# mLSTM and attention block pair: ScalarE takes the turned quarters out of PSUM, VectorE adds the skip part in SBUF

## The chip, the cores and the metric

The kernel runs on one core of one Trainium2 chip, in one launch. The metric is the device time in microseconds (us); the median of several runs counts. All arithmetic is fp32, and large products are made of three fp32r products of high and low parts.

## The reference

A first block and a second block work on a sequence of 1024 positions of 1024 features. The first block normalises its rows, projects them (`w_in`) to four parts, mixes two of them by windowed means, and runs two of them through a bidirectional mLSTM. Its sum goes through `w_out`. The second block (spatial gating, a wide convolution, windowed attention) is not touched by the change.

The part that the change touches is the mLSTM, cut to what matters:

```
c = silu(conv5(u));  q, k = headwise(c);  v = headwise(u)       # 4 heads of 256 features
for both directions, for chunks of 128 positions, with carried state (C, n, m):
    s   = (q k^T) * exp(log_D - m_t)                            # inside the chunk
    num = s v + inter_w * (q C);   den = rowsum(s) + inter_w * (q n)
    h   = num / max(|den|, exp(-m_t))
    C   = decay * C + (ws * k)^T v                              # to the next chunk
h = h_fwd + h_bwd
h = (h - mean(h)) * rsqrt(var(h) + EPS)                         # over a head's 256 features
out = (h * mh_norm_w + skip_w * c) * silu(m_z)
```

## The kernel before

The mLSTM stage works head after head (`units(h)` on each engine), and in a head over 16 units: unit m is chunk pair p = m // 2 in direction d = m % 2. An engine's order is the order of the Python code of its block; engines wait for each other by semaphores alone, and no planner is involved.

In each unit TensorE makes the state product (inter, L1016, into bank 0), then one item that prepares the next head, then the product inside the chunk (intra, L1026, into four half banks in turn) and the two products of the state update (L1033, banks 2 and 3). The items for the next head are twelve pieces of q (L964), turned k (L974) and v (L976) in units 0 to 11 (`FILL`), and two pieces of scores (L987) in units 12 and 14. They all go through one PSUM bank, bank 1, the fill bank: `fill` waits until the last content of the bank has been taken out.

At the end of units 7, 9, 11 and 13 (`TURN`) TensorE also turns a quarter (128 features by 512 positions) of the head before into feature order (`turn_h`, L1001), for heads 0 to 2 through the same fill bank. The head's 1024 rows have been normalised by then: VectorE gathers statistics, ScalarE makes the root in unit 3 (`root`, L1849, which needs another activation table than the exponentials of `weight`), VectorE the reciprocal in `roots` at the end of the pair of units 4 and 5, and ScalarE normalises two chunks in each of units 5 to 8 (`norm_h`, L2035).

Before, ScalarE writes the skip part (`skip_w * c`) of a quarter into a tile `yt` one unit early (`skip_part`, L2018). VectorE reads the turned quarter from the fill bank, scales it and adds `yt`, at the end of its pair of units (`mix_y`, L1480), after totals (L1517), denominators, outputs and state updates (L1496), and with that frees the bank. GpSimd (POOL) multiplies with the gate (`gate_mul`, L630), ScalarE takes the high part (`high_y`, L2029), and POOL the low part (`gate_low`, L638). Two tiles `yt` are used in turn; whoever writes one first waits for the low part of the quarter two before.

ScalarE's order in a unit, before: weight of the next unit (L2008), a row load on its own DMA queue in odd units (`spread`, four pairs of units ahead), evacuation of the state product into `tmpi` or `tmpj` (L2052), root, norms, high part, skip part, and last the evacuation of the fill bank (L1976 q, L1979 k, L1981 v, L1987 scores). POOL's order: masked weight product `Pm` (L651), weighted keys (L617), a mask for the loaded rows (L623), gate product, low part. SP reloads the gate's tile after each gate product; nothing else on SP stands in the change.

The last head's own quarters (12 to 15) are turned after the stage through other banks; their code keeps its order.

Of the kernel before, what the change touches and what calls it, by code (L numbers as in the profile page):

```python
# [9 lines left out]
ALU = mybir.AluOpType  # L10
ACT = mybir.ActivationFunctionType
# [7 lines left out]
HALF = 512  # L19
# [9 lines left out]
NH = 4  # L29
# [77 lines left out]
def build(nc, I, out):  # L107
# [48 lines left out]
    with ctx:  # L156
# [91 lines left out]
        yts = (yt0, yt1)  # L248
# [81 lines left out]
        def head_quarter(n):  # L330


            return (2 * (n // 4) + n % 2, n % 4 // 2) if n >= 12 else (n // 2, n % 2)

        def yt_last(i):
            return hc0[:, 2 * i:2 * i + 2, :].rearrange("p a b -> p (a b)")
# [427 lines left out]
        def _(pe):  # L764
# [186 lines left out]
            def fill(name, value):  # L951


                turns[0] += 1
                return take(free[turns[0] % len(free)], name, value)
# [35 lines left out]
            def turn_h(h, i):  # L991

                n = 4 * h + i
                mt, nh = head_quarter(n)[0] % 2, head_quarter(n)[1]
                pe.wait_ge(s["v_hn"], NT * h + 4 * nh + 4)
                if h < NH - 1:
                    ps = fill("v_y1", n + 1)
                else:
                    ps = ring_x("v_y1", 12 + 2 * i + 1)
                for b in range(4):  # L1000
                    mm = pe.transpose(ps[:, b * P:(b + 1) * P], hcs[h % 2][:, 4 * nh + b, mt * P:(mt + 1) * P],  # L1001
                                      idn)
                mm.then_inc(s["t_h"], 1)
# [242 lines left out]
        def filled(eng, t_name, t_value, name, value):  # L1246

            eng.wait_ge(s[t_name], t_value)
            return bank[bank_of[name, value]]
# [3 lines left out]
        def _(ve):  # L1253
# [210 lines left out]
            def mix_y(h, i):  # L1464
                n = 4 * h + i
                j = V_MH + head_quarter(n)[0]
                if h == NH - 1:

                    ps = filled(ve, "t_h", n + 1, "v_y1", 12 + 2 * i + 1)
                    ve.wait_ge(s["a_t1"], n + 1)  # L1470
                    y = yt_last(i)
                    ve.scalar_tensor_tensor(y, ps[:, :], VT[:, j:j + 1], y, ALU.mult, ALU.add).then_inc(s["v_y1"], 1)
                    ve.wait_ge(s["v_y1"], 12 + 2 * i + 1)
                    ve.wait_ge(s["l_smz"], 16 * 16)
                    ve.tensor_tensor(y, y, smz_last(i), ALU.mult).then_inc(s["v_y1"], 1)
                    return
                ps = filled(ve, "t_h", n + 1, "v_y1", n + 1)
                ve.wait_ge(s["a_t1"], n + 1)
                y = yts[n % 2][:, :]
                ve.scalar_tensor_tensor(y, ps[:, :], VT[:, j:j + 1], y, ALU.mult, ALU.add  # L1480
                                        ).then_inc(s["v_y1"], 1)

            def state(h, n):
                _, p, d, ck, r = unit(n)
# [49 lines left out]
            def units(h):  # L1534
                for q in range(8 * h, 8 * h + 8):
                    n = 2 * q
                    _, p, _, _, r0 = unit(n)
                    r1 = unit(n + 1)[4]
                    total(h, n)
                    state(h, n)  # L1540
                    total(h, n + 1)
                    if p:
                        ve.wait_ge(s["v_tot"], upd_of(h, p - 1, 1) + 1)
                    sums = wide[q % 2][:, :].rearrange("p (d c) -> p d c", d=2)[:, :, HD]
                    chain(ve.tensor_tensor(den[:, 0, :], sums, cols[:, 1, r0:r1 + 1:r1 - r0], ALU.max))
                    chain(ve.scalar_tensor_tensor(den[:, 0, :], sums, -1.0, den[:, 0, :], ALU.mult, ALU.max))
                    chain(ve.reciprocal(den[:, 1, :], den[:, 0, :]))
                    output(h, n)
                    state(h, n + 1)
                    output(h, n + 1)  # L1550
                    if p >= 6:
                        chunk_mean(n - 4)
                        chunk_mean(n - 3)
                    if p >= 5:
                        chunk_stats(h, n - 2)
                        chunk_stats(h, n - 1)
                    if h and p == 0:
                        head_stats(h - 1)
                    if h and p == 2:
                        roots(h - 1)  # L1560
                    if h and n % 16 + 1 in TURN:
                        mix_y(h - 1, TURN[n % 16 + 1])
                if h == NH - 1:
                    head_stats(h)
# [281 lines left out]
        def _(ac):  # L1846
# [117 lines left out]
            def evac_features(h, i):  # L1964

                if i == 0 and h >= 2:
                    ac.wait_ge(s["t_inter"], 14 * (h - 1))
                    ac.wait_ge(s["g_kw"], 14 * (h - 1))
                    ac.wait_ge(s["t_upd"], 14 * (h - 1))
                    ac.wait_ge(s["t_intra"], 16 * (h - 1))  # L1970
                ps = filled(ac, "t_hw", 12 * h + i + 1, "a_hq", 12 * h + i + 1)
                pv = ps[:, :].rearrange("p (t c) -> p t c", t=2)
                t = 2 * (i % 4)
                if i < 4:
                    m, nh = i // 2, i % 2
                    ac.activation(qTs[h % 2][:, m, nh * HALF:(nh + 1) * HALF], ps[:, :], ACT.Copy  # L1976
                                  ).then_inc(s["a_hq"], 1)
                elif i < 8:
                    ac.activation(kts[h % 2][:, t:t + 2, :], pv, ACT.Copy).then_inc(s["a_hq"], 1)  # L1979
                else:  # L1980
                    ac.activation(vs[h % 2][:, t:t + 2, 0:HD], pv, ACT.Copy).then_inc(s["a_hq"], 1)  # L1981

            def evac_scores(h, b):
                if h >= 2:
                    ac.wait_ge(s["g_P"], 16 * (h - 1))
                ps = filled(ac, "t_st", 2 * h + b + 1, "a_st", 2 * h + b + 1)
                ac.activation(STs[h % 2][:, 4 * b:4 * b + 4, :], ps[:, :].rearrange("p (c t) -> p c t", c=4), ACT.Copy  # L1987
                              ).then_inc(s["a_st"], 1)
# [12 lines left out]
            def weight(n):  # L2001
# [4 lines left out]
                if n >= 2:  # L2006
                    ac.wait_ge(s["g_P"], n - 1)
                ac.activation(Wb[:, n % 2, :], brd(q)[:, d, :], ACT.Exp, bias=cols[:, 3, r:r + 1]  # L2008
                              ).then_inc(s["a_W"], 1)

            def skip_part(n):
                j, nh = head_quarter(n)
                y = yts[n % 2][:, :] if n < 12 else yt_last(n - 12)
                if 1 < n < 12:
                    ac.wait_ge(s["g_ymlo"], n - 1)
                if n == 12:
                    ac.wait_ge(s["t_h"], 12)
                ac.activation(y, cc[:, j, nh * HALF:(nh + 1) * HALF], ACT.Copy,  # L2018
                              scale=VT[:, V_SK + j:V_SK + j + 1]).then_inc(s["a_t1"], 1)

            def high_y(n):
# [16 lines left out]
            def units(h):  # L2038
                weight(16 * h)
                for n in range(16 * h, 16 * h + 16):  # L2040
                    _, p, d, _, r = unit(n)
                    m = n % 16
                    if m < 15:
                        weight(n + 1)
                    if n % 2 and n // 2 + 4 < NU // 2:
                        spread(n // 2 + 4)
                    if p:
                        i = upd_of(h, p - 1, d)
                        ps = filled(ac, "t_inter", i + 1, "a_tmp", i + 1)
                        if n >= 4:  # L2050
                            ac.wait_ge(s["v_h"], n - 3)
                        ac.activation(tmps[p % 2][:, d, :], ps[:, 0:AUG], ACT.Copy, scale=cols[:, 0, r:r + 1]  # L2052
                                      ).then_inc(s["a_tmp"], 1)
                    if h == NH - 1 and m == 15:
                        for k in range(12, 16):
                            skip_part(k)
                    if h and m == 3:
                        ac.wait_ge(s["v_lnv"], h)
                        root(sd[:, :], v1_[:, :])
                    if h and m in (5, 6, 7, 8):  # L2060
                        norm_h(h - 1, 2 * m - 10)
                        norm_h(h - 1, 2 * m - 9)
                    if n in GATE_MUL:
                        high_y(GATE_MUL[n])
                    if h and m + 1 in TURN:
                        skip_part(4 * (h - 1) + TURN[m + 1])
                    if h + 1 < NH:
                        for i in FILL.get(m, ()):
                            evac_features(h + 1, i)
                        if m in (12, 14):  # L2070
                            evac_scores(h + 1, (m - 12) // 2)

            for i in range(12):
                evac_features(0, i)
# [213 lines left out]
```

## Time and profile before

| | us |
|---|---|
| median of 3 runs (1312.31 to 1315.47) | 1312.75 |
| the profiled execution | 1309.26 |
| its span, first to last instruction | 1307.5 |
| TensorE busy in the span | 1228.7 (94%) |
| VectorE busy | 651.2 (50%) |
| ScalarE busy | 349.7 (27%) |
| GpSimd busy | 470.7 (36%) |

Shares over the span mix stages with different limits. The mLSTM units run from about 537 to 745 us of the span; what the change touches is read there. PE is TensorE, PEld its weight load, DVE VectorE, ACT ScalarE, POOL GpSimd.

### The profile page before, as it was taken

The page shows a single profiled execution, that of the slowest core. Times are in us where ns is not written, and L with a number is a line of the kernel's source. Part 1 is how long each engine was busy: PE and PEld are TensorE (multiplying, and loading weights), DVE is VectorE, ACT ScalarE, POOL GpSimd, SP SyncE. Part 2 cuts the span into 40 slices and gives each one's busy share as a digit, 9 for nine tenths or more (in the row PEclk, how much of TensorE's full clock was granted, in tenths as well). Part 3 has the DMA queues.
Part 4 walks back from the last instruction along what each step waited for, and adds up shares of the span by engine and source line. Part 5 has one row for each costly group of instructions (what it writes and reads, how often), then busy time and mean ns, then how long its engine had stood idle before and what let it go on. Part 6 is the DMA issues. An engine that isn't in the chain of part 4 may idle for free.

```text
span 1307.5 us, 17484 instructions
## 1 busy us (share of the span) xinstructions
PE 1228.7 (94%) x6744; PEld 1014.2 (78%) x6744; DVE 651.2 (50%) x1234; ACT 349.7 (27%) x710; POOL 470.7 (36%) x449
## 2 busy tenths in 40 slices
PE   4999999999999999998887999879999999999995
PEld 3777878999888788786666799858988886667784
DVE  5324445311556003375556832871798425445568
ACT  6211111000122112546353611131111134443311
POOL 1123212222446111644444554442313225343433
PEclk9999999999999999999899999889999999999998
DMA  6131121343411132101111262051121210050012
GB/s 207 42 137 41 33 73 33 97 155 104 102 34 47 50 109 83 44 24 34 34 33 37 64 207 65 1 205 33 33 81 48 74 33 33 1 185 33 21 61 113
DMA packets 84484, 92.94 MB, mean 71 GB/s; under 512 B 12721, under 2 KB 72329, under 8 KB 84402
## 3 DMA queue, kind: packets, MB, share of 16 engines
q1 hardware_dynamic: 75698, 87.62, 20.6%
q10 hardware_dynamic: 8704, 4.20, 1.1%
q8 instruction: 55, 0.90, 0.3%
q14 instruction: 27, 0.22, 0.1%
HBM read 74.45 MB, written 18.92 MB: 71 GB/s over the span
## 4 chain that ended last, share of the span: by engine, by line
PE 85%; DVE 9%; issue 2%; ACT 1%; POOL 1%; DMA 1%; SPq 1%; DVEq 0%; POOLq 0%; ACTq 0%
PE bank L790 21%; PE bank L791 20%; PE bank L792 20%; PE bank L1016 3%; PE bank L1033 3%; PE wide L1182 2%; PE wide L869 2%; PE bank L1163 2%; PE wide L1172 2%; PE wide L1026 2%; DVE res L1820 1%; PE bank L987 1%; PE bank L976 1%; DVE Cst L1496 1%; PE bank L964 1%
## 5 line engine op out<-in xcount | busy, mean ns | idle before, releaser
L571 POOL CAST whi<-wraw 128x2048 fp32r<-128x2048 f32 x32 | 61.6, 1925 | 476.6 <-PE bank L792 417.6
L790 PE MATMUL bank<-u_hi,wlo 128*128 128x512 f32 x512 | 201.9, 394 | 3.8 <-DVE u_lo L1285 3.8
L792 PE MATMUL bank<-u_hi,whi 128*128 128x512 f32 x512 | 199.4, 389 | 0.0
L791 PE MATMUL bank<-u_lo,whi 128*128 128x512 f32 x512 | 199.3, 389 | 0.0
L573 POOL TENSOR_TENSOR wlo<-wraw,whi 128x2048 fp32r<-128x2048 f32 x33 | 156.7, 4748 | 2.6
L790 PE MATMUL bank<-x_hi,wlo 128*128 128x512 f32 x320 | 128.8, 403 | 6.2 <-issue 4.5
L791 PE MATMUL bank<-x_lo,whi 128*128 128x512 f32 x320 | 125.8, 393 | 0.0
L792 PE MATMUL bank<-x_hi,whi 128*128 128x512 f32 x320 | 125.7, 393 | 0.0
L790 PEld LDWEIGHTS bank<-u_hi,wlo 128*128 128x128 f32 x512 | 96.3, 188 | 26.3 <-DVE u_lo L1285 4.3
L791 PEld LDWEIGHTS bank<-u_lo,whi 128*128 128x128 f32 x512 | 96.3, 188 | 20.3 <-issue 0.7
L792 PEld LDWEIGHTS bank<-u_hi,whi 128*128 128x128 f32 x512 | 96.2, 188 | 20.3
L790 PEld LDWEIGHTS bank<-x_hi,wlo 128*128 128x128 f32 x320 | 60.7, 190 | 27.4 <-issue 13.6
L736 POOL TENSOR_SCALAR sp<-sp,rcx 128x384 f32<-128x384 f32 (+1 forms) x64 | 35.9, 574 | 112.3 <-DVE rcx L1752 112.3
L790 PE MATMUL bank<-whi,yp_lo 128*128 128x256 f32 x256 | 72.8, 285 | 0.0
L791 PE MATMUL bank<-wlo,yp_hi 128*128 128x256 f32 x256 | 72.4, 283 | 0.0
L792 PE MATMUL bank<-whi,yp_hi 128*128 128x256 f32 x256 | 72.4, 283 | 0.0
L792 PEld LDWEIGHTS bank<-x_hi,whi 128*128 128x128 f32 x320 | 60.8, 190 | 13.2
L791 PEld LDWEIGHTS bank<-x_lo,whi 128*128 128x128 f32 x320 | 60.8, 190 | 11.9
L1665 DVE SCALAR_TENSOR_TENSOR wide<-glu,VT,wide 128x1024 f32<-128x1024 f32 x58 | 69.3, 1282 | 0.0
L790 PE MATMUL bank<-whi,ym_lo 128*128 128x256 f32 x240 | 68.6, 286 | 0.2 <-ACT tmpj L2052 0.2
L791 PE MATMUL bank<-wlo,ym_hi 128*128 128x256 f32 x240 | 68.1, 284 | 0.0
L792 PE MATMUL bank<-whi,ym_hi 128*128 128x256 f32 x240 | 68.0, 283 | 0.0
(321 smaller groups left out, 2541.3 us busy)
## 6 DMA issues: line engine op xcount, KB each, us to landing
wraw<-in_w_in SPq DMA_DIRECT2D x27, 1024.0 KB, 5.4
wraw<-in_w_out SPq DMA_DIRECT2D x12, 1024.0 KB, 5.3
xr<-in_x SPq DMA_DIRECT2D x8, 512.0 KB, 6.8
hst<-in_x SPq DMA_DIRECT2D x4, 1024.0 KB, 5.7
hpool<-hst SPq DMA_DIRECT2D x4, 1024.0 KB, 8.3
smz<-mzs SPq DMA_DIRECT2D x16, 256.0 KB, 2.0
wraw<-nmax ACTq DMA_DIRECT2D x32, 128.0 KB, 3.0
resid<-h SPq DMA_DIRECT2D x8, 512.0 KB, 8.6
```

What stands on the lines that cost most here:

```text
L571: g_.tensor_copy(whi[w % 2][:, :, :], wraw[:, :, :]).then_inc(s["w_hi"], 1)
L573: g_.tensor_tensor(wlo[w % 2][:, :, :], wraw[:, :, :], whi[w % 2][:, :, :].bitcast(F32), ALU.subtract).then_inc(s["w_lo"], 1)
L736: g_.tensor_scalar(row, row, rcx[:, x % 2, i:i + 1], 0.5 if g else 1.0, ALU.mult, ALU.mult).then_inc(s["g_nm"], 1)
L790: pe.matmul(ps, al, bh, start=(k == 0), stop=False)
L791: pe.matmul(ps, ah, bl, start=False, stop=False)
L792: return pe.matmul(ps, ah, bh, start=False, stop=(k == nk - 1))
L869: mm = pe.matmul(ps[:, :], pw[:, g % 2, k, dt * P:(dt + 1) * P], px[:, k, PAD + nh * HALF:PAD + (nh + 1) * HALF], start=(k == 0), stop=(k ...
L1016: mm = pe.matmul(ps[:, 0:AUG], q[:, k, ck * P:(ck + 1) * P], Cst[:, d, k, :], start=(k == 0), stop=(k == 1))
L1026: pe.matmul(ps[:, 0:AUG], Pm[:, n % 2, :], v[:, ck, :], start=True, stop=True).then_inc(s["t_intra"], 1)
L1033: mm = pe.matmul(ps[:, 0:AUG], kwb[:, m % 2, k * P:(k + 1) * P], v[:, ck, :], start=True, stop=True)
L1163: pe.matmul(ps[:, 0:nb * P], qT2[ko:ko + 64, p, n * P:(n + 1) * P], keys[ko:ko + 64, lo * P:(lo + nb) * P], start=True, stop=True).then_in ...
L1665: ins = ve.scalar_tensor_tensor(dst, src, w, acc, ALU.mult, ALU.add)
```

## The change

ScalarE now takes the turned quarters 0 to 11 out of the fill bank with the scale `mh_norm_w` and writes `yt` (`turned_h`), at the end of the unit that turned the quarter. VectorE adds the skip part to `yt`, from `cc` in SBUF, at its old place. ScalarE evacuates the fill bank right behind the state product, ahead of root, norms and high part. The root moves from unit 3 to unit 2, and VectorE's `roots` from the third pair of units to the second. Quarters 12 to 15 keep the old way.

```diff
@@ TensorE, turn_h
-                    ps = fill("v_y1", n + 1)
+                    ps = fill("a_t1", n + 1)
@@ VectorE, mix_y
-                ps = filled(ve, "t_h", n + 1, "v_y1", n + 1)
+                jt, nh = head_quarter(n)
                 ve.wait_ge(s["a_t1"], n + 1)
                 y = yts[n % 2][:, :]
-                ve.scalar_tensor_tensor(y, ps[:, :], VT[:, j:j + 1], y, ALU.mult, ALU.add
-                                        ).then_inc(s["v_y1"], 1)
+                ve.scalar_tensor_tensor(y, cc[:, jt, nh * HALF:(nh + 1) * HALF], VT[:, V_SK + jt:V_SK + jt + 1], y,
+                                        ALU.mult, ALU.add).then_inc(s["v_y1"], 1)
@@ VectorE, units
-                    if h and p == 2:
+                    if h and p == 1:
                         roots(h - 1)
@@ ScalarE
+            def turned_h(n):
+                j = V_MH + head_quarter(n)[0]
+                if n > 1:
+                    ac.wait_ge(s["g_ymlo"], n - 1)
+                ps = filled(ac, "t_h", n + 1, "a_t1", n + 1)
+                ac.activation(yts[n % 2][:, :], ps[:, :], ACT.Copy, scale=VT[:, j:j + 1]).then_inc(s["a_t1"], 1)
+
             def skip_part(n):
                 j, nh = head_quarter(n)
-                y = yts[n % 2][:, :] if n < 12 else yt_last(n - 12)
-                if 1 < n < 12:
-                    ac.wait_ge(s["g_ymlo"], n - 1)
                 if n == 12:
                     ac.wait_ge(s["t_h"], 12)
-                ac.activation(y, cc[:, j, nh * HALF:(nh + 1) * HALF], ACT.Copy,
+                ac.activation(yt_last(n - 12), cc[:, j, nh * HALF:(nh + 1) * HALF], ACT.Copy,
                               scale=VT[:, V_SK + j:V_SK + j + 1]).then_inc(s["a_t1"], 1)
@@ ScalarE, units
+                    if h + 1 < NH:
+                        for i in FILL.get(m, ()):
+                            evac_features(h + 1, i)
+                        if m in (12, 14):
+                            evac_scores(h + 1, (m - 12) // 2)
                     if h == NH - 1 and m == 15:
                         for k in range(12, 16):
                             skip_part(k)
-                    if h and m == 3:
+                    if h and m == 2:
                         ac.wait_ge(s["v_lnv"], h)
                         root(sd[:, :], v1_[:, :])
...
-                    if h and m + 1 in TURN:
-                        skip_part(4 * (h - 1) + TURN[m + 1])
-                    if h + 1 < NH:
-                        for i in FILL.get(m, ()):
-                            evac_features(h + 1, i)
-                        if m in (12, 14):
-                            evac_scores(h + 1, (m - 12) // 2)
+                    if h and m in TURN:
+                        turned_h(4 * (h - 1) + TURN[m])
```

## Rows read from the trace of the kernel before

**Rows 1.** The page's chain that ended last: share of the span by engine.

```profile
PE 85%; DVE 9%; issue 2%; ACT 1%; POOL 1%; DMA 1%; SPq 1%; DVEq 0%; POOLq 0%; ACTq 0%
```

**Rows 2.** Windows, heads 0 to 3: stretch, length, busy by engine, granted clock, DMA.

```profile
536.90:581.00 44.10, 43.85 (x232) 37.38 (x232) 28.80 (x86) 19.21 (x45) 19.79 (x41) 1.00 0.09 25
581.00:643.60 62.60, 51.95 (x248) 42.38 (x248) 35.58 (x107) 30.36 (x64) 28.64 (x48) 0.92 0.12 34
643.60:705.70 62.10, 49.99 (x246) 40.59 (x246) 35.38 (x107) 29.55 (x63) 29.40 (x47) 0.95 0.12 35
705.70:745.40 39.70, 35.01 (x160) 27.98 (x161) 33.13 (x101) 22.23 (x47) 26.62 (x44) 1.00 0.12 34
```

**Rows 3.** Waits in the stage: who for whom, us in total, times, longest.

```profile
PE bank L987 <- DVE yt L1480: 9.0, 4, 2.5
...
PE bank L974 <- ACT kt L1979: 6.0, 2, 3.0
...
PE bank L976 <- DVE yt L1480: 4.1, 4, 1.3
```

**Rows 4.** Timeline of TensorE in head 1, unit 9: start, length, what.

```profile
610.98 1.03 PE L1016 MATMUL bank<-Cst,qT 128*128 128x257 f32 x4
611.85 1.05 PE L976 MATMUL bank<-bdh,um 128*128 128x128 f32 x8
612.74 0.60 PE L1026 MATMUL wide<-v,Pm 128*128 128x257 f32 x2
...
614.04 0.60 PE L1001 MATMUL bank<-cst,hc 128*128 128x128 f32 x4
614.48 1.03 PE L1016 MATMUL bank<-Cst,qT 128*128 128x257 f32 x4
```

**Rows 5.** Timeline of head 1, ScalarE's first norms and VectorE's second add.

```profile
598.49 1.09 ACT L2035 ACTIVATE hc<-hc,nmr,rs 128x256 f32<-128x256 f32 x2 [3.46 <-DVE nmr L1455]
...
616.00 0.74 DVE L1480 SCALAR_TENSOR_TENSOR yt<-bank,VT,yt 128x512 f32<-128x512 f32 x1
```

**Rows 6.** Lines by shape, ScalarE: count, busy us, mean ns, idle before.

```profile
L1864 ACT ACTIVATE u_hi<-wide,VT 128x512 fp32r<-128x512 f32 x16 | 10.4, 689 | 1.9 <-PE wide L843 1.7
...
L1979 ACT ACTIVATE kt<-bank 128x512 f32<-128x512 f32 x14 | 8.3, 590 | 0.0
```

**Rows 7.** Timeline around the root, heads 1 and 3.

```profile
586.54 0.60 ACT L1976 ACTIVATE qT<-bank 128x512 f32<-128x512 f32 x1 [0.38 <-PE bank L964]
...
587.63 0.36 DVE L1509 TENSOR_SCALAR v_<-mv 128x8 f32<-128x8 f32 x1
...
589.20 1.28 ACT L1849 ACT_TABLE_LOAD   x1
...
590.67 1.03 PE L1016 MATMUL bank<-Cst,qT 128*128 128x257 f32 x4
...
712.75 0.63 DVE L1509 TENSOR_SCALAR v_<-mv 128x8 f32<-128x8 f32 x1
...
714.42 0.42 DVE L1517 TENSOR_TENSOR wide<-wide,tmpj 128x257 f32<-128x257 f32 x1
```

**Rows 8.** VectorE at 128x512 (ns min/median/max), POOL's wait and longest operation.

```profile
L1347 DVE TENSOR_TENSOR yp_lo<-yr,yp_hi x16: 679/688/3042, 79.9 to 237.2; 128x512 fp32r<-128x512 f32 x16
...
L1480 DVE SCALAR_TENSOR_TENSOR yt<-bank,VT,yt x12: 730/740/743, 607.9 to 744.3; 128x512 f32<-128x512 f32 x12
...
POOL yt L630 <- DVE yt L1480: 17.1, 10, 2.2
...
L638 POOL TENSOR_TENSOR ym_lo<-yt,ym_hi 128x512 fp32r<-128x512 f32 x11 | 14.2, 1291 | 6.1 <-ACT ym_hi L2029 6.1
```

**Rows 9.** Timeline of head 3: ScalarE's first norms, VectorE's total behind them.

```profile
722.13 1.09 ACT L2035 ACTIVATE hc<-hc,nmr,rs 128x256 f32<-128x256 f32 x2 [3.16 <-DVE nmr L1455]
...
723.98 0.43 DVE L1517 TENSOR_TENSOR wide<-wide,tmpj 128x257 f32<-128x257 f32 x1 [1.88 <-ACT tmpj L2052]
...
726.22 0.43 DVE L1517 TENSOR_TENSOR wide<-wide,tmpj 128x257 f32<-128x257 f32 x1 [1.04 <-ACT tmpj L2052]
```

## The prediction, written before the result was known

> **What bounds the kernel now.** The page comes first: TensorE makes 85% of the chain that ended last [rows 1]. An average over the span says little here, because the change touches one stage only, so the stage is cut by heads, each from its first intra product to the next head's [rows 2]. The reader is to compare the four windows. Head 0, which has neither turned quarters nor row norms, takes 44.1 us, and TensorE is busy in 43.85 of them at full granted clock (1.00): TensorE is its pace. Heads 1 and 2 do the same work plus four turned quarters of the head before and take 62.6 and 62.1 us; TensorE is idle for 10.65 and 12.1 us of them, and its clock is granted at 0.92 and 0.95. Head 3 has no next head to fill and takes 39.7 us.
>
> The list of waits names the idle time [rows 3]: scores (L987) and values (L976) wait for VectorE's L1480, which empties the one fill bank of the turned quarter, 13.1 us in eight waits, and the turned keys (L974) wait 6.0 us in two for a ScalarE evacuation (L1979).
>
> The order of time shows why. TensorE's turn starts at 614.04 [rows 4], VectorE reaches the bank at 616.00 and frees it at 616.74 [rows 5]: 2.70 us, since the add stands at the end of a pair's chain (totals, denominators, states, outputs). And at 598.49 ScalarE has idled 3.46 us in front of two norms, which stand ahead of the key evacuation, so TensorE stands about 3 us (half of the 6.0).
>
> **The change part by part.**
>
> *The bank goes to ScalarE.* Twelve adds of 0.74 us that read PSUM on VectorE become twelve scaled copies that read PSUM on ScalarE, and twelve scaled copies from SBUF (L2018) go there. A scaled PSUM copy of 128x512 is in the trace at 0.69 (L1864), an unscaled one at 0.59 (L1979) [rows 6]. I take 0.69; ScalarE's work in count stays what it is. What counts is when the bank comes free. A unit without a gap gives the pieces [rows 4]: state product (inter) 0.87, fill 0.89, intra and update 1.30, turn 0.44. After the first turned unit's fill ends, TensorE has 1.30 + 0.44 = 1.74 us to the end of the turn, then the next state product of 0.87 in another bank, so the bank is wanted at 2.61. ScalarE evacuates the fill (0.59) and does two norms (1.09 [rows 5]), 1.68, waits for the turn and copies to 1.74 + 0.69 = 2.43. That is 0.18 early, so this edit's wait goes to nothing; the later turns have no norms and more room. Behind the waiting copy stand the next unit's weight, state evacuation and fill evacuation. The weight has a unit's lead (intra needs it about 2 us later), and the other two need TensorE work that also comes after the turn: nothing more waits.
>
> *The fill evacuation moves ahead of root, norms and high parts.* No instruction is added and none issues a DMA. It makes TensorE's release independent of the norms; the norms and the high parts come at most one evacuation (0.59) later, and the consumer of the high part, a POOL subtraction, has a unit of room.
>
> *Root and reciprocal earlier.* VectorE's two small instructions move by a pair of units, so the norms at unit 5 find their factor ready; some 3.3 us of ScalarE idling goes in each head. The root itself moves past one weight, one row load and one state evacuation on ScalarE. The row load is for four pairs on, so no one waits for it. The state evacuation holds the next state product and VectorE's total. In head 1 the root's table load stands at 589.20 now; the evacuation that it will follow ends at 587.14 [rows 7], and VectorE's variance (587.63 + 0.36) is ready before the load ends. So load, root and the load back (2 x 1.28 and about 0.2) end at 589.9, the weight (0.4) follows, and the state evacuation (0.47) ends near 590.7, where the next state product starts now, 590.67 [rows 7]. That leaves nothing, or 1.3 (one table load) if the load only starts once the variance is there; I take 0.3 for each of heads 1 and 2. In head 3 no fill evacuation lies ahead, so the root must wait for the variance at 713.4 (712.75 + 0.63), the load back ends near 714.9, the weight near 715.3, and the state evacuation comes at about 715.2; VectorE's total goes from 714.42 [rows 7] to 715.7. Price 1.3.
>
> *The skip part on VectorE in SBUF.* The operation takes both large operands from SBUF, a form this stage doesn't show at 128x512. The nearest row, L1347, also has two SBUF operands and ranges from 0.68 (median 0.69) to 3.04 [rows 8], so the bounds are 0.06 less than now and, with POOL's longest operation here (1.29, L638 [rows 8]) in the way, 1.3 more. I take the median, 0.69. In heads 1 and 2 it lies beside TensorE's work: a pair with a turn takes TensorE 3.06 + 3.50 = 6.5 us, and VectorE's share of such a head is 35.6 us over eight pairs, 4.4 each [rows 2]. POOL waits for it ten times of twelve, 17.1 us in all [rows 8], so POOL is mostly quiet just then. In head 3 VectorE is the pace (33.1 of 39.7 us busy [rows 2]), so there it is on the path: 4 x (0.69 - 0.74), nothing, up to 4 x 1.3 = 5.2 more if POOL is in the way each time.
>
> The spread of L1347 is a case for a rule. The Trainium skill, "SBUF — State Buffer", section "Who interferes with whom", says that a VectorE instruction with two SBUF inputs contends with a GpSimd instruction that reads SBUF, and that the later one stands until the first is done. The trace agrees in kind (0.68 at best, 3.04 at worst, against adds with one PSUM input, which keep to 0.73 to 0.74 throughout [rows 8]). By row the sum gets nothing for it; by the rule it gets what the third rival below works out.
>
> **The sum.** From first intra product to first intra product head 0 takes 44.1, head 1 62.6, head 2 62.1 [rows 2]. Without the waits heads 1 and 2 are head 0 with four turns: 44.1 + 4 x 0.44 = 45.9, plus 0.3 for the root and 0.2 at the head's end, where the last high part still waits for the last gate product: 46.4. Gains 16.2 and 15.7. These are larger than the named waits because they hold products made at the lower of the clock's two levels after idle stretches (a granted mean of 0.92 in head 1, where TensorE is busy 51.95 us for work worth 43.85 + 1.76 [rows 2]) and the wait at the head's end that follows from a late last add. Head 3: VectorE idles 1.88 us before 723.98 for a state evacuation held by the norms that began at 722.13 [rows 9], and 1.04 before 726.22 [rows 9]; 2.9 goes, 1.3 comes: 1.6. Together 16.2 + 15.7 + 1.6 = 33.5. What follows (the output projection, its loads, POOL's splits) is released by this stage's own semaphores and shifts as a whole. The profiled execution took 1309.26 (span 1307.5): 1275.8. The median of the runs, 1312.75, is 3.5 above it, so I forecast 1279.
>
> **The rivals.**
>
> *Only the named waits go.* The pace in heads 1 and 2 passes to VectorE's chain per pair, which keeps the clock low and the wait at the head's end. For it: 35.6 us of VectorE's work in a head of 46.4 would be 77%, and its steps in a pair depend on one another. Against it: head 0 runs at TensorE's pace with the same chain. Then 9.0 + 4.1 + 6.0 = 19 us [rows 3]: 1294.
>
> *The norms still wait.* The root's own wait and two table loads eat what the earlier place gives; the stalls of L974 and the idling in head 3 stay, 6.0 + 2 of clock and 2: about 10 less, 1289. Against it: the variance is ready more than 10 us before the norms (587.99 [rows 7] against 598.49 [rows 5]).
>
> *Two SBUF inputs meet POOL.* In head 3 POOL is busy 26.6 of 39.7 us, 67% [rows 2]. An add that meets its longest operation of 1.3 waits half of it on average, 0.65; 4 x 0.67 x 0.65 = 1.7: 1281.
>
> *Slower.* ScalarE's queue is in order, and the copy stands behind norms, high parts and their waits. Place: the fill bank after each turn. VectorE frees it now 2.70 us after the turn's start [rows 4, 5]; the copy does so at 0.44 + 0.69 = 1.13 if ScalarE is free. If ScalarE ran 1.6 us late, the bank would gain nothing, and from there each us late costs 8 us over the eight turns of heads 1 and 2. With 3.5 late: 8 x 1.9 = 15 lost against 8 won by the norms, so 1320. Against it: ScalarE is busy 30.4 of 62.6 us [rows 2], and 30.4 of 46.4 is still 65%.
>
> **How the numbers follow.** Forecast 0.70 (its own range 1274 to 1285: 37 us when every TensorE gap goes, 28 with the upper bounds of root and add). Named waits only 0.14, norms still wait 0.02, POOL in the way 0.08, slower 0.06, of which 0.02 near its point of balance with today's time. A measurement of this kernel can tell about 0.3% (4 us) from no change. Faster 0.70 + 0.14 + 0.02 + 0.08 = 0.94, same 0.02, slower 0.04. The range reaches from 1273 to the first rival, 1294.
>
> **What would show it.** Right: no TensorE wait on VectorE's `yt`, none of L974 on L1979; the granted clock of heads 1 and 2 at 0.99 or more; firsts of intra 46 to 47 us apart; ScalarE's copy of the turned quarter at 0.69 and within 1.3 us of the turn's start; no ScalarE wait for `nmr`. Wrong: TensorE waiting at L976 or L987 for ScalarE's `yt` or for VectorE's states; adds far over 0.7 beside POOL; a ScalarE stretch of 2 us or more before the root in heads 1 and 2.

## The result, and the profile after

The changed kernel takes 1283.4 us (median of 4 runs, 1282.51 to 1284.05); the kernel before, run beside it, takes 1312.53 (4 runs, 1311.08 to 1315.47). The ratio is 0.9775, with a 95% interval of 0.9756 to 0.9793: 29.1 us less. The forecast was 1279, with a range of 1273 to 1294.

The profiled execution took 1283.93 us, its span 1282.1. The profile page's chain of waits by engine answers to [rows 1]: VectorE's share falls from 9% to 7%.

```profile
PE 86%; DVE 7%; POOL 3%; issue 2%; ACT 1%; SPq 1%; DMA 1%; ACTq 0%; POOLq 0%; DVEq 0%
```

The windows of heads 0 to 3, with the columns of [rows 2] (stretch, length, busy time and count of PE, PEld, DVE, ACT and POOL, granted clock, DMA share, GB/s):

```profile
540.65:584.78 44.13, 43.86 (x232) 37.39 (x233) 28.82 (x86) 19.23 (x45) 19.81 (x41) 1.00 0.09 25
584.78:632.71 47.93, 46.92 (x248) 38.47 (x249) 35.22 (x108) 30.89 (x64) 29.54 (x48) 1.00 0.15 42
632.71:681.60 48.89, 46.46 (x247) 37.95 (x247) 35.22 (x107) 29.96 (x63) 30.25 (x47) 1.00 0.16 46
681.60:720.09 38.49, 35.09 (x161) 27.88 (x161) 33.00 (x101) 21.74 (x47) 27.93 (x44) 1.00 0.12 36
```

Head 0, which the change doesn't touch, is what it was. Heads 1 and 2 get 14.7 and 13.2 us shorter, head 3 1.2. The stage falls from 208.5 to 179.4 us, and these 29.1 are the whole gain: after the stage both profiles take 562 us (562.1 and 562.0). The two spans differ by 25.4 only because what comes ahead of the stage took 540.65 us in this execution and 536.9 in that of before, in code that is the same.

TensorE's idle time in heads 1 and 2 fell from 10.65 and 12.1 us to 1.0 and 2.4, and the granted clock is 1.00 in both. The waits of the stage (who for whom, us in total, times, longest) that answer to [rows 3] and to POOL's in [rows 8]:

```profile
POOL yt L630 <- DVE yt L1480: 5.9, 5, 1.7
...
ACT yt L2016 <- PE bank L1001: 5.4, 10, 0.8
...
PE wide L1026 <- POOL Pm L651: 4.7, 6, 1.9
...
PEld bank L987 <- issue: 1.7, 4, 0.4
...
PEld bank L976 <- ACT yt L2016: 1.4, 4, 0.4
...
PE bank L1016 <- ACT tmpj L2056: 0.8, 2, 0.5
```

No wait of scores or values for VectorE is left and none of the turned keys. What is left of the fill bank is 1.4 us of weight loads for the values that wait for ScalarE's copy, and 1.7 us in front of the scores' weight loads, for which the profile names no releaser ("issue"). These four loads stand behind the turns of units 11 and 13; in head 1 the first begins at 620.41, 0.11 after the copy's end (619.61 + 0.69), so they are the bank's too. The largest TensorE wait is now that for `Pm`.

The bank's release in the first turned unit of head 1, in order of time (start, length, engine, line), answers to [rows 4, 5]:

```profile
604.82 1.08 ACT L2039 ACTIVATE hc<-hc,nmr,rs 128x256 f32<-128x256 f32 x2
...
605.43 0.60 PE L1001 MATMUL bank<-cst,hc 128*128 128x128 f32 x4
...
605.87 1.03 PE L1016 MATMUL bank<-Cst,qT 128*128 128x257 f32 x4
606.07 0.69 ACT L2016 ACTIVATE yt<-bank,VT 128x512 f32<-128x512 f32 x1 [0.17 <-PE bank L1001]
...
606.81 0.97 PEld L976 LDWEIGHTS bank<-bdh,um 128*128 128x128 f32 x8 [0.31 <-ACT yt L2016]
606.81 1.16 PE L976 MATMUL bank<-bdh,um 128*128 128x128 f32 x8
```

The copy ends at 606.76, 1.33 us after the turn began; VectorE's add ended 2.70 after it. In this unit TensorE gets the bank within a tenth of a microsecond of wanting it (606.81 against 606.74, the state product's start plus 0.87).

### The profile page after: what moved, and what is told of

Its sections match the earlier page's. It is cut to its first block, busy times and chain, and to the rows that moved or that the text cites. A ratio compares the mean times of both kernels' runs of the same rounds, so it can differ in the third digit from the quotient of the medians.

```text
span 1282.1 us, 17482 instructions
## 1 busy us (share of the span) xinstructions
PE 1224.2 (95%) x6744; PEld 1012.1 (79%) x6744; DVE 651.2 (51%) x1234; ACT 350.0 (27%) x710; POOL 473.5 (37%) x449
## 4 chain that ended last, share of the span: by engine, by line
PE 86%; DVE 7%; POOL 3%; issue 2%; ACT 1%; SPq 1%; DMA 1%; ACTq 0%; POOLq 0%; DVEq 0%
PE bank L790 22%; PE bank L791 21%; PE bank L792 21%; PE bank L1016 3%; PE bank L1033 3%; PE wide L1182 2%; PE wide L869 2%; PE bank L1163 2%; PE wide L1172 2%; PE wide L1026 2%; DVE res L1820 1%; PE bank L987 1%; PE bank L976 1%; POOL ym_lo L638 1%; DVE res L1836 1%
```

## The experiments

The theory: TensorE was held in two ways, by the time at which the turned quarter left the fill bank and by norms that stood in ScalarE's queue waiting for a root. The clock's lower level followed from both. Rivals: the order of ScalarE's evacuations is what pays; VectorE's load is what pays (the engine counts, not the time of release); one wait only hid another. Times are medians beside runs of the kernel before on the same chip. A time can tell about 4 us, so smaller effects are read from the heads' lengths in the traces, one trace per run; the heads 1 to 3 together took 164.4 us before and 135.3 after.

**Parts alone, on the kernel before.**

*e1_evac_first: only the evacuation's place.*

```diff
                         ac.activation(tmps[p % 2][:, d, :], ...).then_inc(s["a_tmp"], 1)
+                    if h + 1 < NH:
+                        for i in FILL.get(m, ()):
+                            evac_features(h + 1, i)
+                        if m in (12, 14):
+                            evac_scores(h + 1, (m - 12) // 2)
...
                         skip_part(4 * (h - 1) + TURN[m + 1])
-                    if h + 1 < NH:
-                        (the same block)
```

> The kernel before with one part of the change: ScalarE evacuates the fill bank right behind the state product. VectorE still empties the turned quarter, the root stays in unit 3. My theory: the turned keys of unit 6 no longer wait for the norms, but the next state product does (its evacuation stands behind them), so some 2.5 us in each of heads 1 and 2 and nothing in head 3: 1307.5, with TensorE's 13 us of waits for VectorE's yt unchanged. Rival (the order of the evacuations is what pays): 1290 or less, and the waits for yt shrink.

Measured: 1309.98 beside 1309.55, ratio 0.9996 (0.9977 to 1.0014). Heads 1 to 3 get 2.0 us shorter in all. The waits of its stage show why:

```profile
PE bank L987 <- DVE yt L1480: 9.0, 4, 2.5
...
PE bank L976 <- DVE yt L1480: 5.4, 4, 1.4
PE bank L1016 <- ACT tmpj L2052: 5.0, 4, 1.8
```

The 6.0 us of the turned keys [rows 3] are gone. In their place the state product (L1016) of heads 1 and 2 stands 3.0 us (the other 2.0 of its 5.0 are in head 3 and were there before), and the values wait 1.3 us more for `yt`: the waiting norms now hold the next state evacuation instead of the key evacuation. A wait behind which another engine stands is not cured by changing what stands behind it.

*e2_root_early: only the root and the reciprocal.*

```diff
-                    if h and p == 2:
+                    if h and p == 1:
                         roots(h - 1)
...
-                    if h and m == 3:
+                    if h and m == 2:
                         ac.wait_ge(s["v_lnv"], h)
```

> The kernel before with the root in unit 2 and the reciprocal at the end of the second pair, nothing else. My theory: ScalarE's 10 us of waiting for nmr go, TensorE's 6.0 us at L974 go, and with the clock after them about 5 us in heads 1 and 2 and 1 in head 3: 1301.5; the waits for yt stay at 13 us. Rival (the norms are hidden behind the waits for yt that follow): within 4 us of the kernel before.

Measured: 1300.77, 0.9932 (0.9914 to 0.9950), 8.8 us less; heads 1 to 3 get 11.6 shorter in its trace. Its head 1:

```profile
585.75:642.58 56.83, 49.08 (x248) 39.88 (x248) 35.21 (x108) 30.28 (x64) 28.66 (x48) 0.97 0.13 38
```

The wait of the turned keys on the matmul side is gone, the eight on L1480 stand as they were (9.0 and 4.3). Against [rows 2], TensorE's idle time in heads 1 and 2 falls by 2.9 us each (the named 6.0), its busy time by 2.9 and 1.5, with the granted clock at 0.97 in both instead of 0.92 and 0.95, and head 3 by 1.45.

*e3_both_orders: e1 and e2 together.*

> Everything of the change but the engine: evacuation first and root early, VectorE still empties the bank at the end of its pair. My theory: the two orders solve the same wait, so together they give no more than the early root alone, 1301; what is left to the changed kernel, some 18 us, is the bank. Rival (the order pays): under 1290.

Measured: 1300.67, 0.9926 (0.9905 to 0.9947): e2's time. The two orders deal with the same wait, and the rival that ScalarE's order pays for itself falls. Its heads 1 and 2:

```profile
584.93:641.65 56.72, 48.73 (x249) 40.04 (x249) 35.21 (x108) 30.71 (x64) 28.65 (x48) 0.97 0.14 38
641.65:699.20 57.55, 48.16 (x247) 39.57 (x247) 35.02 (x107) 29.80 (x63) 29.37 (x47) 0.97 0.13 38
```

TensorE still idles 8.0 and 9.4 us, at a granted clock of 0.97: what is left to the changed kernel, 17.2 us in heads 1 to 3, is the bank.

*e4_add_sooner: e3, and VectorE keeps the bank but adds sooner.* The mix stands ahead of the pair's second state update, its second output and the statistics instead of behind them.

```diff
+                    if h and n % 16 + 1 in TURN:
+                        mix_y(h - 1, TURN[n % 16 + 1])
                     state(h, n + 1)
...
-                    if h and n % 16 + 1 in TURN:
-                        mix_y(h - 1, TURN[n % 16 + 1])
```

> As the run with both orders, and VectorE's scaled add from PSUM stands ahead of its second state update instead of at the pair's end, some 1.2 us sooner and ahead of the statistics; the engine and the operation stay. My theory: what counts is when the bank comes free, not which engine does it; the add would end some 1.5 us after the turn's start against 2.7 to 3.8 now, and most of the 18 us come: 1287, waits for yt under 3 us in total. Rival (ScalarE's hand matters, because VectorE's chain is the pace): 1297 or more, with new TensorE waits for VectorE's states (L1496).

Measured: 1288.97, 0.9838 (0.9821 to 0.9856), 20.6 us less. Head 1 and head 3, and head 1's second turn:

```profile
587.42:636.20 48.78, 47.09 (x248) 38.46 (x248) 35.20 (x108) 30.69 (x64) 28.56 (x48) 1.00 0.15 44
...
685.84:725.59 39.75, 35.45 (x161) 27.88 (x161) 32.89 (x101) 21.77 (x47) 27.56 (x44) 1.00 0.12 35
```

```profile
615.02 0.60 PE L1001 MATMUL bank<-cst,hc 128*128 128x128 f32 x4
...
615.81 0.74 DVE L1480 SCALAR_TENSOR_TENSOR yt<-bank,VT,yt 128x512 f32<-128x512 f32 x1
```

The add ends 1.53 us after the turn's start (2.70 before, 1.33 with ScalarE's copy), and heads 1 to 3 take 138.2. So, by the heads' lengths, the two orders (in the main the early root) make 11.9 of the 29.1 us (164.4 to 152.5), the time of release 14.3 (152.5 to 138.2) and the step to ScalarE 2.9 (138.2 to 135.3): turned units of 3.68 to 4.69 instead of 3.89 to 4.98 us, and 1.26 in head 3, where e4's add stands ahead of a state update. This last step also frees the bank 0.20 sooner, so what the engine alone is worth isn't separated. The rival that VectorE's load pays falls for heads 1 and 2: most of the gain comes with the add still on VectorE.

The times split less clearly. They give 8.9 us to e3 and 11.7 more to e4; from e4 to the changed kernel the ratios, taken on two chips (0.9838, and 0.9782 for after_again), leave about 7, good to some 4. Up to 1.7 of that can be head 0 (the last section). So 2.9 may be too low for the last step.

**Parts undone or moved, on the changed kernel.**

*e5_old_root: root and reciprocal at their old place* (the two lines of e2 turned round).

> The changed kernel with the root back in unit 3 and the reciprocal at the end of the third pair. My theory: the norms wait for nmr again, but behind the evacuation of the fill bank, so only the next state product is held: from the unit lengths of the run with the evacuation first alone, 1.9 us more in each of heads 1 and 2 and 1.1 in head 3, so 5 us slower than the changed kernel. Rival (with the bank on ScalarE a late norm also delays the copy of the first turned quarter and the clock falls): 10 us or more slower.

Measured: 1290.73, 0.984 (0.9811 to 0.9870); heads 1 to 3 take 140.1, 4.8 more. Units 3 to 6 of head 1 take 2.60, 3.32, 2.61 and 4.36 us instead of 2.89, 2.90, 2.61 and 2.61. So the early root is worth 4.8 us here, and 9.9 where VectorE empties the bank (e1 against e3, 162.4 and 152.5): in e5 the granted clock of heads 1 and 2 is 1.00, in e1 it is 0.94. What a part is worth depends on the parts that are already there.

*e6_root_unit3: the reciprocal early, the root back in unit 3* (only the line with `m == 2`).

> The changed kernel with the root back in unit 3, but VectorE's reciprocal stays at the end of the second pair. My theory: the early reciprocal is what frees the norms; the root in unit 2 holds the third state evacuation by two table loads and costs 0.6 us in heads 1 and 2 and about 1 in head 3. Back in unit 3 it costs 0.2 per head: 1.5 us faster than the changed kernel, seen in units 3 and 4 of the trace (2.6 and 2.8 us in place of 2.9 and 2.9). Rival: VectorE waits for the later root in its second pair and the units 4 and 5 grow: slower by 1 to 3.

Measured: 1284.31, 0.9794 (0.9775 to 0.9812), not to be told from the changed kernel. Head 3 gains 0.97; its root had waited 0.36 for the variance and no longer does, and the rest of the gain isn't explained. Heads 1 and 2 take 0.13 longer each, with 2.60 and 3.31 in units 3 and 4 instead of 2.89 and 2.90. The gain is half of what I expected: in heads 1 and 2 the two table loads cost the same wherever they stand.

*e10_evac_last: the fill evacuation back behind the high part.* The block of e1, put just ahead of `turned_h`.

> The changed kernel with ScalarE's evacuation of the fill bank back behind root, norms and high part (but ahead of the turned copy, which needs it). My theory: with the early root nothing in front of it waits long; only in unit 7 do the norms make the turn wait 0.45 us, so about 1 us slower than the changed kernel in heads 1 and 2 together. Rival (evacuation first is what lets ScalarE hold the pace): each of the units 5 to 13 grows by the 1.08 of norms or 0.6 of the high part, 10 us or more slower.

Measured: 1285.3, 0.9791 (0.977 to 0.9812); heads 1 and 2 take 0.9 us more together, unit 7 alone 0.57 each. This part of the change is worth 1 us.

*e11_more_vector: one more VectorE operation ahead of each add* (row statistics of the same `cc` quarter, whose result is not used).

```diff
+                q = cc[:, jt, nh * HALF:(nh + 1) * HALF]
+                mark(ve.bn_stats(scr[:, :], q))
                 ve.scalar_tensor_tensor(y, cc[...], ...)
```

> The changed kernel with one statistics operation of 0.7 us more on VectorE ahead of each of the twelve adds; its result is not used. My theory: VectorE's add lies beside TensorE in heads 1 and 2, apart from about 0.6 us at each head's end, and on the path in head 3 (4 x 0.7): 4 us slower in all. Rival (VectorE is near the pace in heads 1 and 2 as well): 0.7 us for each of eight units more, 8 us or more. Second rival (hidden everywhere): no change in any head.

Measured: 1288.89, 0.9811 (0.979 to 0.9831). Heads 1 and 2 take 0.5 us more each, all of it at the head's end; head 3 takes 1.73 more. The start of its head 3 (one line further down in this kernel, L1027 and L1034):

```profile
685.48 0.72 PE L1027 MATMUL wide<-v,Pm 128*128 128x257 f32 x2 [2.36 <-DVE hc L1534]
686.00 1.92 PE L1034 MATMUL bank<-v,kwb 128*128 128x257 f32 x4
```

The state update's products take 1.92 us there and 1.03 in the changed kernel: TensorE is at the lower level of its clock (granted 0.69 from 685.48 to 690.98), and unit 1 takes 0.61 more. So only 1.1 of the 1.73 stand in the units of the adds, where four operations of 0.68 put in 2.7. In heads 1 and 2 VectorE's work lies beside TensorE's but for the last quarter, as forecast; in head 3 it is on the path, but for less than half of its length.

*after_again: the changed kernel once more, for the comparison on this chip.*

> The changed kernel once more, on the same chip as the three others, so that they are compared with it directly. All theories: 29 us faster than the kernel before, with the unit lengths of the first trace (turned units 3.68 to 3.74 and 4.69 us).

Measured: 1284.58, 0.9782 (0.9759 to 0.9806); heads 1 to 3 take 135.3 again.

**Towards a better version.**

*e7_turn_inside: the turn between the two products of the state update* (behind the first, instead of behind the second), so that it ends sooner before the next fill.

```diff
+                            if h and k == 0 and n % 16 in TURN:
+                                turn_h(h - 1, TURN[n % 16])
...
-                    if h and n % 16 in TURN:
-                        turn_h(h - 1, TURN[n % 16])
```

> The changed kernel with TensorE's turn between the two products of the state update. The bank comes free 0.43 us sooner against the next fill. My theory: the turned units of heads 1 and 2 are 0.18 to 0.30 us longer than their products because ScalarE's copy ends just after the fill wants the bank; they go from 3.68 to 3.74 us to 3.50 and from 4.69 to 4.39: 2 us faster in all. Rival (the extra is the matmul's own start after a change of operands, or the state of VectorE): no change in these units.

Measured: 1283.04, 0.9788 (0.9767 to 0.9808). Turned units take 3.60, 3.60, 4.49 and 4.39 us instead of 3.68, 3.68, 4.69 and 4.69, but the head's end takes 0.22 more, since the high part there now waits for the gate product. Head 3 takes 1.7 us longer, at a lower granted clock (the last section).

*e8_weight_first: at a head's end the next weight ahead of the last high part.*

```diff
-                weight(16 * h)
+                if h == 0:
+                    weight(0)
...
+                    if m == 15 and h + 1 < NH:
+                        weight(n + 1)
                     if n in GATE_MUL:
                         high_y(GATE_MUL[n])
```

> The changed kernel with the next head's first weight ahead of the last high part on ScalarE, in unit 15. My theory: the 2.24 and 2.45 us between the last intra product of heads 1 and 2 and the first of the next wait for weight, then POOL's product, and the high part stands ahead with 0.52: these go to about 1.75 and 1.95, 1 us faster in all. Rival (POOL's gate product or low part sets the head's end): no change there, or the second unit of the next head grows by as much.

Measured: 1281.93, 0.9776 (0.9755 to 0.9796); heads 1 and 2 get 0.51 and 0.53 us shorter, which was expected; only the trace can tell it. The order of time at the end of head 1, first the changed kernel, then e8:

```profile
631.04 0.62 ACT L2033 ACTIVATE ym_hi<-yt 128x512 fp32r<-128x512 f32 x1
...
631.56 0.68 ACT L2008 ACTIVATE Wb<-wraw,cols 128x128 f32<-128x128 f32 x2
...
632.20 0.46 POOL L651 TENSOR_TENSOR Pm<-ST,Wb 128x128 f32<-128x128 f32 x1 [0.57 <-ACT Wb L2008]
...
632.71 0.70 PE L1026 MATMUL wide<-v,Pm 128*128 128x257 f32 x2 [0.79 <-POOL Pm L651]
```

```profile
627.71 0.39 ACT L2008 ACTIVATE Wb<-wraw,cols 128x128 f32<-128x128 f32 x1
...
628.00 0.62 ACT L2033 ACTIVATE ym_hi<-yt 128x512 fp32r<-128x512 f32 x1
628.36 0.46 POOL L651 TENSOR_TENSOR Pm<-ST,Wb 128x128 f32<-128x128 f32 x1
...
628.87 0.70 PE L1026 MATMUL wide<-v,Pm 128*128 128x257 f32 x2 [0.27 <-POOL Pm L651]
```

The weight, `Pm` and the first intra product of the next head come half a microsecond sooner once the high part (0.62) no longer stands ahead of the weight.

*e9_all: e7, e8, and the root in unit 3 for the last head alone.*

```diff
-                    if h and m == 2:
+                    if h and m == (3 if h == NH - 1 else 2):
```

> The changed kernel with three edits together: the turn between the two products of the state update, the next head's first weight ahead of the last high part, and the root in unit 3 for the last head only. Where each works on another unit, the savings read from the single runs' units add: 1.4 us in the turned units, 1.0 at the heads' ends (the 0.2 that the turn's place cost there goes too), 1.0 in head 3: 3.4 us faster than the changed kernel on the same chip. Rival (the gaps move to the next wait): within 1.5 us of it.

Measured: 1280.87, 0.9760 (0.9738 to 0.9782). Its heads 1 to 3 take 132.0 us, 3.3 less than in the changed kernel:

```profile
584.30:631.27 46.97, 46.39 (x248) 38.54 (x248) 35.16 (x107) 30.92 (x64) 28.67 (x48) 1.00 0.14 41
631.27:678.89 47.62, 45.83 (x246) 38.02 (x247) 35.26 (x106) 30.67 (x63) 29.47 (x47) 1.00 0.16 46
678.89:716.29 37.40, 34.61 (x160) 28.12 (x161) 33.51 (x102) 21.91 (x47) 27.58 (x44) 1.00 0.14 43
```

Its heads 1 to 3 are the shortest of all traces, and its median is the lowest (e8 has the shorter span, 1278.1 against 1278.9, with head 0 at 44.1 instead of 45.8). Against the changed kernel on the same chip (0.9782, 0.9759 to 0.9806) the intervals overlap, so that it is faster by the time alone isn't shown.

## Why the prediction was right, and where the 4.4 us went

*What bounds the kernel: right.* The two waits named were the two causes: e2 takes the one away, e4 the other, and nothing outside the stage changed.

*Gains larger than the named waits: right.* The first rival (named waits only, 1294) fell with the granted clock: 1.00 in heads 1 and 2 where it was 0.92 and 0.95. Two of the signs named beforehand came out against the forecast, by little: TensorE's loads do wait at L976 for ScalarE's `yt` (1.4 us), and heads 1 and 2 take 47.9 and 48.9 us, not 46 to 47.

*The step that was mis-sized: "That is 0.18 early, so this edit's wait goes to nothing".* The heads 1 to 3 came to 135.3 us where the forecast's own terms make 130.9 (46.4 + 46.4 + 38.1). The difference of 4.4 is that between 1279 and 1283.4, and the units' lengths place it:

| term | forecast | measured | us missed |
|---|---|---|---|
| turned units over 3.50 and 4.39, four each in heads 1 and 2 | 0 | 0.18 to 0.30 each | 2.0 |
| root in units 3 and 4, heads 1 and 2 | 0.3 each | 0.58 each | 0.6 |
| head's end over head 0's 1.73 | 0.2 each | 0.51, 0.72 | 0.8 |
| head 2's first two units over head 0's | 0 | 0.64 | 0.6 |
| head 3 | -1.6 | -1.2 | 0.4 |

The first term: I let the turn end where the next product begins, 0.44 after its start. The row of the turn lasts 0.60 [rows 4], and the copy starts 0.64 after the turn's start (606.07 against 605.43). With that in the working, the copy ends at 1.30 + 0.64 + 0.69 = 2.63, the bank is wanted at 2.61, and the slack of 0.18 was never there. A fill that waits also begins with a weight load that lies beside no earlier product (above, load and product both start at 606.81; in the unit of [rows 4], which has no wait, the load starts at 611.63 and the product 0.22 later). So its eight products take 1.16 instead of 1.05: 0.07 of lateness and 0.11 of that make the 0.18. The four fills of scores begin 1.09 instead of 0.87 after the state product and take 0.08 longer, which makes the 0.30. e7 ends the turn sooner: its scores begin at 0.87 again, and 1.4 of the 2.0 us come back.

The root: the working had the next weight and state evacuation 0.4 and 0.47 behind the second load. In head 1:

```profile
590.91 1.28 ACT L1849 ACT_TABLE_LOAD   x1
...
592.20 0.21 ACT L1849 ACTIVATE sd<-v_ 128x8 f32<-128x8 f32 x1
...
592.43 1.28 ACT L2008 ACT_TABLE_LOAD   x1
...
594.03 0.46 ACT L2056 ACTIVATE tmpj<-bank,cols 128x257 f32<-128x257 f32 x1
594.59 0.43 DVE L1517 TENSOR_TENSOR wide<-wide,tmpj 128x257 f32<-128x257 f32 x1 [1.91 <-ACT tmpj L2056]
```

The load stands ahead of the root's own input, as I worked out (it begins at 590.91, VectorE's variance at 591.39), so the upper end of 1.3 didn't come; but the sequence holds two units by 0.29 each, and VectorE's total by 1.91. The norms (L2039) no longer wait for `nmr` in any head.

The head's end: the last high part stands ahead of the next head's weight, and e8 shows that this is 0.5 of it per head. Head 2's first units wait for `Pm` behind a POOL subtraction; they did so before, and head 0 as the model of a head without waits doesn't have it.

Head 3: 2.9 was to go and 1.3 to come. Unit 6 fell from 4.51 to 2.50, which is 2.0; the early root costs 0.97 (e6). Idle time of VectorE was taken at its full length, where the unit on TensorE got shorter by less.

Two bounds of the forecast's own range don't come out as written, without bearing on the forecast: 37 us less than 1312.75 is 1276, not 1274, and with both upper bounds (2.0 for the root, 5.2 for the adds) 26.3 of the 33.5 are left, not 28.

*The skip part in SBUF: right in kind, 0.05 too low.* The adds take 0.74 in the median, no less than with PSUM (0.69 was taken). The shortest takes 0.732, so the 0.05 is the operation's own length and no meeting with POOL. Such meetings lengthen a few. The lines by form (ns min, median, max) of VectorE's adds and POOL's weighted keys, after:

```profile
L1480 DVE SCALAR_TENSOR_TENSOR yt<-cc,VT,yt x12: 732/741/930, 607.4 to 719.0; 128x512 f32<-128x512 f32 x12
```

```profile
L617 POOL TENSOR_SCALAR kwb<-kt,cols x56: 467/478/1010, 540.6 to 714.6; 128x256 f32<-128x256 f32 x56
```

Before, the adds kept to 730 to 743 [rows 8] and the weighted keys to 498 at most. In order of time, head 3:

```profile
707.05 1.29 POOL L638 TENSOR_TENSOR ym_lo<-yt,ym_hi 128x512 fp32r<-128x512 f32 x1
707.96 0.93 DVE L1480 SCALAR_TENSOR_TENSOR yt<-cc,VT,yt 128x512 f32<-128x512 f32 x1
708.30 0.90 POOL L651 TENSOR_TENSOR Pm<-ST,Wb 128x128 f32<-128x128 f32 x1
```

The add that begins beside POOL's subtraction takes 0.19 longer, and POOL's 0.46 product behind it takes 0.90. A stand to the end of the first one's row would be 0.38 and 0.59; what each takes longer is 0.19 and 0.44. The trace thus agrees in kind with the Trainium skill, "SBUF — State Buffer", section "Who interferes with whom" (VectorE with two SBUF inputs and a GpSimd instruction that reads SBUF hold each other up, the later one standing until the first is done), but the price is small and most of it falls on POOL: five weighted keys of 0.91 to 1.01 and two products of 0.90 and 0.91 make about 3.2 us there. Twelve adds of 774 ns on average instead of 737 make 0.44 us in all. The third rival priced 0.65 per add in head 3; the adds there come to at most 0.93.

*The slower rival fell.* ScalarE's own queue hardly holds the copy: ten of the twelve copies wait for TensorE's turn (5.4 us), among them all eight of heads 1 and 2, and start 0.64 to 0.70 after its start; the other two, in head 3, come straight behind ScalarE's high part, 0.76 after it. In e10 the fill evacuation stands late in its queue again, and that costs 0.9 us over both heads, not the 15 us of this rival.

## What to carry to other kernels

Where one bank passes between engines, write the release as a time after the producer's start, and take the producer's end from its row's length, not from the start of the next one: a slack of 0.18 us on paper was one of -0.02. Look first for what an engine's queue holds while it waits (the norms that waited for a root): making the awaited value earlier paid 8.8 us here (4.8 once the bank came free early), and changing the order behind the wait paid nothing that the time shows. Release time came before the choice of engine: by the heads' lengths 14.3 of the gain, by the times 11.7, could be had by moving one VectorE instruction, on top of the two orders.

## What the runs showed of the hardware that was not expected

*The clock's lower level doesn't follow from the same idle time each time.* Head 0 is the same code in all kernels and took 44.1 us in eight of the fourteen traces and 45.8 in six. TensorE's first products there in the changed kernel, and in its second profile (after_again):

```profile
540.65 0.70 PE L1026 MATMUL wide<-v,Pm 128*128 128x257 f32 x2 [1.93 <-POOL Pm L651]
541.19 1.05 PE L1033 MATMUL bank<-v,kwb 128*128 128x257 f32 x4
542.08 1.02 PE L964 MATMUL bank<-cc,Amat 128*128 128x512 f32 x2
```

```profile
542.54 0.70 PE L1026 MATMUL wide<-v,Pm 128*128 128x257 f32 x2 [1.92 <-POOL Pm L651]
543.08 1.59 PE L1033 MATMUL bank<-v,kwb 128*128 128x257 f32 x4
544.46 1.91 PE L964 MATMUL bank<-cc,Amat 128*128 128x512 f32 x2
```

After the same idle time (1.93 and 1.92 us) the two products of the fill took 1.02 us in one execution and 1.91 in the other, whose granted clock over the head is 0.96 instead of 1.00. That is 1.7 us which belongs to no edit; it is why head 0 is left out of the sums above.

The length of the idle time counts all the same. Taken over the starts of heads 0 and 3 in the fourteen traces, none of the eighteen that follow at most 1.86 us of it is slowed; of the ten that follow 1.90 to 2.36 us eight are (their first two units take 0.6 to 2.1 us longer), and two, both behind 1.93, aren't. Two of the eight are at head 3's start: in e7 behind 2.06 us (granted clock 0.92 over the head, 40.19 us instead of 38.49) and in e11 behind 2.36, where the changed kernel has 1.85. There the edit itself had made the idle time longer, so the 1.7 us of e7's head 3 may be a price of the edit; one trace can't tell. What decides near 1.9 us wasn't found, and no run set out to vary this time.

*A table load doesn't wait for what its activation waits for.* In all three heads it begins before the variance is written (in head 1 at 590.91, against 591.39 for the start of VectorE's operation). In head 3 it has ended (687.19 + 1.28 = 688.47) before the variance is there (688.79), and the root waits 0.36 us instead of a load's 1.28.
